# Two latent feed-forward norms rooted from sums that are gathered during the output projection, with the residual addition on GpSimd

## The reference, cut to what matters

```python
x = x + g1 * rmsnorm_2(y_lat, norm_g[l, 1])
x = x + g2 * rmsnorm_2(swiglu(modulate(x, norm_g[l, 2], sh2, sc2), ffn_w_in[l], ffn_w_out[l]),
                       norm_g[l, 3])
```

## Time and profile before

| | |
|---|---|
| median of 3 runs | 3146.11 us (3144.01 to 3150.38) |
| profiled execution, its own time | 3146.42 us |
| its span | 3144.5 us |
| busy PE; DVE; ACT; POOL | 3064.0 us (97%); 1814.2 (58%); 1188.8 (38%); 1241.6 (39%) |
| chain that ended last | PE 87%, DVE 8%, ACT 3%, issue 1%, POOL 1% |
| TensorE clock, mean | 0.99 of 2.4 GHz |

### The profile page before, as it was taken

The page is one execution under the profiler, slowest core; times in us unless marked ns, Lnnn a source line. Parts: engine busy times, 40 slices in busy tenths (PEclk is TensorE's granted clock), DMA queues, the critical chain, the costliest instruction groups (busy, mean ns, idle before and its releaser), DMA issues.

```text
span 3144.5 us, 41638 instructions
## 1 busy us (share of the span) xinstructions
PE 3064.0 (97%) x16512; PEld 2544.4 (81%) x16512; DVE 1814.2 (58%) x2858; ACT 1188.8 (38%) x1836; POOL 1241.6 (39%) x568
## 2 busy tenths in 40 slices
PE   8999999999999999999999999999999999999998
PEld 7658888886589888778888998878888788878887
DVE  3556777845553664666337877567786458352224
ACT  4544212235544432324336555542223435332222
POOL 4304444533157343334344454434444320134442
PEclk9999999999999999999999999999999999999999
DMA  7204554623135222223333333435653210123331
GB/s 130 77 14 118 169 164 129 196 67 82 36 111 167 87 75 88 80 67 108 108 101 101 111 113 106 134 111 171 191 160 117 82 61 14 41 71 100 98 95 67
DMA packets 480432, 323.87 MB, mean 103 GB/s; under 512 B 102520, under 2 KB 447744, under 8 KB 479728
## 3 DMA queue, kind: packets, MB, share of 16 engines
q1 hardware_dynamic: 475472, 309.60, 33.7%
q10 hardware_dynamic: 2656, 6.30, 0.5%
q0 software_dynamic: 2112, 5.32, 0.5%
HBM read 315.90 MB, written 5.24 MB: 102 GB/s over the span
## 4 chain that ended last, share of the span: by engine, by line
PE 87%; DVE 8%; ACT 3%; issue 1%; POOL 1%; DMA 0%; DVEq 0%; ACTq 0%; POOLq 0%
PE G L2854 13%; PE G L2863 12%; PE G L2864 12%; PE G L2868 12%; PE G L3082 6%; PE G L3083 5%; PE G L3087 5%; PE G L2880 3%; PE G L3944 1%; PE G L3299 1%; POOL WL L749 1%; PE SS L3210 1%; PE G L3236 1%; ACT WH L808 1%; PE G L3289 1%
## 5 line engine op out<-in xcount | busy, mean ns | idle before, releaser
L749 POOL TENSOR_TENSOR WL<-raw,WH 128x1024 fp32r<-128x1024 f32 (+1 forms) x520 | 1218.9, 2365 | 1796.8 <-ACT WH L808 1796.8
L808 ACT ACTIVATE WH<-raw 128x1024 fp32r<-128x1024 f32 (+1 forms) x520 | 492.1, 994 | 580.7 <-PE G L3087 397.1
L2863 PE MATMUL G<-hH,WH 128*128 128x512 f32 x1520 | 595.9, 392 | 0.0
L2864 PE MATMUL G<-hL,WH 128*128 128x512 f32 x1520 | 592.8, 390 | 0.0
L2868 PE MATMUL G<-hH,WL 128*128 128x512 f32 x1520 | 359.9, 389 | 0.0
L2863 PEld LDWEIGHTS G<-hH,WH 128*128 128x128 f32 x1520 | 285.9, 188 | 60.7 <-ACT t_s L1289 0.8
L2864 PEld LDWEIGHTS G<-hL,WH 128*128 128x128 f32 x1520 | 286.0, 188 | 58.8
L2868 PEld LDWEIGHTS G<-hH,WL 128*128 128x128 f32 x1520 | 285.3, 188 | 59.2
L1723 DVE SCALAR_TENSOR_TENSOR acc<-adaw,cvec,acc 128x512 f32<-128x512 f32 x280 | 250.8, 949 | 4.2
L2854 PE MATMUL G<-hH,WH 128*128 128x512 f32 (+1 forms) x432 | 166.9, 386 | 0.0
L2854 PE MATMUL G<-hL,WH 128*128 128x512 f32 (+1 forms) x432 | 164.3, 380 | 0.0
(11 more groups left out here) (777 smaller groups left out, 6197.2 us busy)
## 6 DMA issues: line engine op xcount, KB each, us to landing
raw<-ffn_w_in_in SPq DMA_DIRECT2D x264, 256.0 KB, 3.4
adaw<-ada_w_in SPq DMA_DIRECT2D x48, 1024.0 KB, 5.3
raw<-ab_w_in_in SPq DMA_DIRECT2D x128, 256.0 KB, 3.0
raw<-ffn_w_out_in SPq DMA_DIRECT2D x96, 256.0 KB, 2.9
raw<-w_gate_in SPq DMA_DIRECT2D x88, 256.0 KB, 3.3
raw<-w_up_in SPq DMA_DIRECT2D x88, 256.0 KB, 3.4
raw<-w_down_in SPq DMA_DIRECT2D x64, 256.0 KB, 2.8
raw<-w_in_in SPq DMA_DIRECT2D x40, 256.0 KB, 3.3
```

Of the source, the lines that this page charges most:

```text
L749: nc.gpsimd.tensor_tensor(WL[c % 2][:, cut], raw[c % 2][:, cut], WH[c % 2][:, cut].bitcast(F32), ALU.subtract)\
L808: nc.scalar.activation(WH[c % 2][:, cut], raw[c % 2][:, cut], ACT.Copy).then_inc(weights_hi, 1)
L2863: mm(dst, view(WH[c % 2], k), high, start=(k == 0 and not (joint and i)), stop=False)
L2864: mm(dst, view(WH[c % 2], k), low, start=False, stop=False)
```

## The change

It rewrites what stands between o7 and gu1 at both places:

- The three sums of the formula above are gathered while o0 to o7 are made. ACT squares y as before and also squares G y (`y1.c`, with the gain as scale); DVE multiplies x, gain and bank (`y1.b`) and adds the three running totals in PSUM banks (M[1], M[0], S[0]), for k = 1 to 6. `last_out` puts the column products of the totals (12 of the program's) into o7, ahead of its last three matmuls.
- `fresh_columns` adds the last tile's three column products behind o7, spreads the first root, does 8 keep-awake matmuls and spreads the second root. ACT takes the second root (`root_of_fresh`) from sums that DVE puts together in five 128 x 4 operations. sum x^2 (`squared_x`) is kept from the norm that each layer began with, by a copy.
- The new x is no longer needed for the sums. DVE makes the update tiles (`d1`), POOL adds them to xT (`fresh_rows`, between the low parts of gu0 and of gu1 in its order), DVE makes h and hL. The three are interleaved, two updates ahead.
- `opening` has no keep-awake matmuls of its own at the two places. At m the 32 transposes and 8 copies to xtok move into the opening, in two banks instead of four, and gu1 waits for the last copy. `late` (WH of gu1) moves ahead of the seventh tile.
- `rows_back` is issued ahead of the last head tiles. SP waits for POOL's eighth addition instead of `t.x1.7`.

```diff
@@ GpSimd
+            def fresh_rows(n):
+                for k in range(KD):
+                    pool.wait_ge(dve_done, at("dve", f"{n}.d1.{k}"))
+                    nc.gpsimd.tensor_tensor(xT[:, k, :], xT[:, k, :], ht[:, k % 2, :], ALU.add).then_inc(x_added, 1)
+            seam = first["t.o"] + 5
+            low_parts(cut2, seam)
+            fresh_rows("t")
+            low_parts(seam, cut3)
@@ SP
-                    sp.wait_ge(dve_done, at("dve", "t.x1.7"))
+                    sp.wait_ge(x_added, FRESH_ROWS["t"] + KD)
@@ ScalarE
+            def root_of_fresh(n):
+                act.wait_ge(dve_done, at("dve", f"{n}.n2.var"))
+                nc.scalar.activation(ncol[:, 12:16], squared_x[:, int(n == "m"), :], ACT.Sqrt, bias=eps[:, 0:1], scale=1.0 / D)\
+                    .then_inc(act_done, did("act", f"{n}.n2.root"))
@@ ScalarE, projected, behind the square of y
+                        if k >= 3:
+                            act.wait_ge(dve_done, at("dve", f"{n}.y1.cad{k - 2}"))
+                        nc.scalar.activation(five_rows[n][:, k % 2, :] if k else S[0][:, :], y[:, k, :], ACT.Square, scale=mcols[:, passes[n][0], 1, k:k + 1])\
+                            .then_inc(act_done, did("act", f"{n}.y1.c{k}"))
@@ ScalarE
+            rows_back()
             latent_heads()
-            projected("t", PT_.y, T, KD, ((1, rows_back),))
+            projected("t", PT_.y, T, KD)
@@ VectorE, fresh_sums
+                    V.scalar_tensor_tensor(product if k else M[0][:, :], x[:, k, :], gain(n, 1)(k), out_bank(n, k)[:, :], ALU.mult, ALU.mult)\
+                        .then_inc(dve_done, did("dve", f"{n}.y1.b{k}"))
+                    if inner:
+                        V.tensor_tensor(M[1][:, :] if k < KD - 2 else rstd[:, :], M[1][:, :], sq[:, k % 2, :], ALU.add)
+                        V.tensor_tensor(M[0][:, :] if k < KD - 2 else five_rows[n][:, 3, :], M[0][:, :], product, ALU.add)
+                        V.tensor_tensor(S[0][:, :] if k < KD - 2 else five_rows[n][:, 2, :], S[0][:, :], five_rows[n][:, k % 2, :], ALU.add)
@@ VectorE, fresh_normed
+                dve.wait_ge(pe_done, at("pe", f"{n}.y1.bc"))
+                update(0)
+                dve.wait_ge(act_done, at("act", f"{n}.n2.root"))
+                V.reciprocal(ncol[:, 8:12], ncol[:, 12:16]).then_inc(dve_done, did("dve", f"{n}.n2.rec"))
+                update(1)
+                dve.wait_ge(pe_done, at("pe", f"{n}.n2.bc"))
+                for k in range(KD):
+                    dve.wait_ge(x_added, FRESH_ROWS[n] + k + 1)
+                    if k >= 2:
+                        dve.wait_ge(dve_done, at("dve", f"{n}.n2.L{k - 2}"))
+                    V.scalar_tensor_tensor(scaled_rows(f"{n}.n2", ht, k, T), x[:, k, :], gx(k), S[0][:, :], ALU.mult, ALU.mult).then_inc(dve_done, did("dve", f"{n}.n2.h{k}"))
+                    if k + 2 < KD:
+                        update(k + 2)
+                    if k >= 1:
+                        rest(k - 1)
+                rest(KD - 1)
@@ TensorE, opening
-                keep_busy(n, 8)
+                if n not in ("t.n2", "m.n2"):
+                    keep_busy(n, 8)
...
+                    if n == "m.n2":
+                        turned_residual(k)
@@ TensorE
+            def fresh_columns(n):
+                keep_busy(f"{n}.y1", 4)
+                pe.wait_ge(act_done, at("act", f"{n}.y1.sq{KD - 1}"))
+                column_of(M[0], 0, sq[:, (KD - 1) % 2, :], False, True).then_inc(pe_done, did("pe", f"{n}.y1.sum"))
+                pe.wait_ge(dve_done, at("dve", f"{n}.y1.b{KD - 1}"))
+                column_of(S[1], 0, five_rows[n][:, 4, :], False, False)
+                pe.wait_ge(act_done, at("act", f"{n}.y1.c{KD - 1}"))
+                column_of(S[1], 4, five_rows[n][:, (KD - 1) % 2, :], False, True).then_inc(pe_done, did("pe", f"{n}.y1.sums"))
+                pe.wait_ge(dve_done, at("dve", f"{n}.y1.rec"))
+                to_all(M[1][:, :], 0).then_inc(pe_done, did("pe", f"{n}.y1.bc"))
+                keep_busy(f"{n}.n2", 8)
+                pe.wait_ge(dve_done, at("dve", f"{n}.n2.rec"))
+                to_all(S[0][:, :], 8).then_inc(pe_done, did("pe", f"{n}.n2.bc"))
```

More of the change, by code:

```diff
@@ L300, in __init__ @@
                 self.last, self.part = last, part
+                self.five_at = last - size([P, 5, N])
                 row = size([P, N])
@@ L852, in stats, with rounded @@
                 root(n, cols // P, K * P)
-            def rounded(n, K, H, free, cols=T, shift=None, k0=0, temp=ht, late=None):
+            def rounded(n, K, H, free, cols=T, shift=None, k0=0, temp=ht, late=None, late_at=None, then=None):
                 for k in range(k0, K):
-                    if k == (0 if n in IN_BANKS and n != "b0.n1" else 2) and late is not None:
+                    if k == (late_at or (0 if n in IN_BANKS and n != "b0.n1" else 2)) and late is not None:
                         hi(late)
@@ L865, in rounded @@
                         nc.scalar.activation(H[:, k, 0:cols], scaled_rows(n, temp, k, cols), ACT.Copy).then_inc(act_done, did("act", f"{n}.H{k}"))
+                    if then and k >= 2:
+                        then(k - 2)
+                if then:
+                    then(K - 2)
+                    then(K - 1)
             def feed_forward(n, silu=silu, N=T, between=iter(()), last=None):
@@ L1523, in second_half @@
                 n, N = ps.n, ps.N
[L1524 to L1536, removed]
+                root_of_fresh(n)
+                rounded(f"{n}.n2", KD, hH, f"{n}.o{KD - 1}", N, shift(n, 3), late=first[f"{n}.o"] + 5, late_at=6, then=kept_tokens if n == "m" else None)
                 feed_forward(n, ps.silu, N, between, (f"{n}.y2", lambda n, k: (ps.y2[:, k, :], lambda k: act.wait_ge(dve_done, at("dve", f"{n}.down3.{k}")))))
@@ L2353, in second_half @@
+            def second_half(ps, x, p, y1, between=iter(())):
                 n, N = ps.n, ps.N
-                mean(f"{n}.n2", N)
-                normed(f"{n}.n2", KD, lambda k: x[:, k, :], gain(p, 2), hH, hL, N, shift(p, 3))
+                fresh_sums(n, x)
+                fresh_normed(n, y1, x)
                 feed_forward(n, ps.y2, N, ps.FH, ps.FL, ps.silu, fresh=True, between=between, last=f"{n}.y2")
@@ L3043, in feed_forward @@
                         else:
+                            if n == "m" and t == 1:
+                                pe.wait_ge(act_done, at("act", f"m.xt{KD - 1}"))
                             streamed(c, groups)
```

120 lines of the change are left out of this document (93 added, 27 removed).

## The result

| | before | after |
|---|---|---|
| median | 3146.33 us (20 runs, 3142.49 to 3151.84) | 3151.91 us (20 runs, 3146.69 to 3155.76) |
| profiled execution; its span | 3146.42; 3144.5 | 3154.8; 3153.0 |
| ratio, 95% interval | | 1.0018 (1.0012 to 1.0024) |
| busy PE; DVE; ACT; POOL | 3064.0; 1814.2; 1188.8; 1241.6 | 3066.7; 1831.4; 1187.8; 1262.3 |
| chain that ended last | PE 87%, DVE 8%, ACT 3% | PE 88%, DVE 8%, ACT 2% |

What follows compares the result with a forecast made beforehand. PE, busy 97% of the span, was taken to bound the kernel. 8.6 - 0.2 + 6.5 - 1.3 - 0.3 = 13.3 us less than 3146.4 gave 3133, range 3129.5 to 3138.5.

Steps and rivals of the forecast that it cites:

- Equal times elsewhere: Outside the two places and the longer o7, the new profile would show the same times as before.
- 0.2 us at t, 1.3 at m: Loss from the lower clock in the openings after PE's wait: 0.2 us (at most 1) and 1.3 (0 to 3).
- 8.6 were forecast: Place t, o7's added products included: 28.0 us against 36.6, 8.6 us less, before the clock's loss.
- 6.5 ahead of the clock's 1.3: Place m, with transposes and copies in the opening: 30.8 us against 37.3, 6.5 less, before the clock's loss.
- The first h can start at 8.0: Behind o7 at each place: column products, two spreads and keep-awake products let DVE start the first h at 8.0 us.
- Inside o7, 2.5 us: Three groups of column products ahead of o7's last three matmuls cost 2.5 us on the path at each place.
- The cycle, 2.10: On DVE in the openings, one cycle of h, update, hL takes 2.10 us, bounds 1.98 and 2.34; before, 1.44.
- The mechanism at m: ACT's tile copies and WH make hH6 and hH7 late; gu1 waits for the last copy, at 28.3 us.
- POOL's additions at 1.27 us, not waited for, and DVE not slowed beside them: Eight additions of 1.27 us fit DVE's 2.1 us cycle; the rival of mutual blocking would give 3153.
- The old rows, 0.3 us: Rows fetched earlier shift ACT's queue and DVE's hL row ahead of t: 0.3 us lost, between 2 gained and 0.8 lost.
- SP's later release delays nothing: Released at about 22.8 us behind z instead of 17.5, gu2's weights still come in time, with 5 us cover.
- the clock stays at 1.2 GHz: Rival: low clock through the whole opening at both places, 8.3 us slower, 3154; most of slower's 0.04.

Runs made afterwards that it cites:

- e4: The changed kernel with its new 32-byte tile at the end of memory, every tile of before where it lay: 3138.73 us, ratio 0.9973.
- e1: The kernel before with one unused 32-byte tile ahead of the large tiles, no instruction differing: 3157.74 us, ratio 1.0034.
- e6: As e4, with 14 keep-awake products ahead of the opening at both places: 3136.23 us, ratio 0.9971.
- e7: As e4, with o7's 12 column products put one behind each of its last 12 matmuls: 3136.46 us, ratio 0.9975.
- e8: e6 and e7 together, with 4 keep-awake products instead of 8 between the two spreads: 3131.65 us, ratio 0.9956.
- e9: As e8, with the third update ahead of the first h: 3134.12 us, ratio 0.9959.
- e12: The kernel of e9 run once more, unchanged: 3135.65 us, ratio 0.9965.
- e10: As e4, with the residual additions on VectorE (DVE) instead of GpSimd, one ahead of each h: 3148.46 us, ratio 1.0013.
- e3: The changed kernel with 96 unused bytes behind its new tile, large tiles on multiples of 128 again: 3152.31 us, ratio 1.0016.

## Why the prediction was wrong, point by point

- **"Equal times elsewhere": wrong, and this turned the sign.** The new 32-byte tile was not priced at all. It cost 11 to 14 us (14 by the changed kernel's ratio 1.0018 against e4's 0.9973; 13.2 in the rows of the three untouched stretches; 10.7 when done alone, e1). With it taken out the kernel ran in 3138.7, just above the range's end.
- **The clock, "0.2 us at t, 1.3 at m": right for the openings, and the larger loss was missed.** It was put into the opening alone, behind PE's wait of 3.6 us. The wait came as predicted (3.57); at m the clock fell there and cost 1.7 us (e4 against e6), and at t, where it fell there in e7, it cost nothing. But the clock also fell ahead of the wait, under column products and spreads, where each microsecond of PE delays h0, and this stood in the sum at nothing. At t that made 12.55 of 8.0 in the changed kernel and in e4, and 9.7 in e6, with the clock low for a third of the time; at m it made 9.74, and 0.9 more in o7.
- **What the places missed, added up.** At t, 8.6 were forecast ahead of the clock's 0.2 and 2.8 came: 4.6 went to the late h0, 1.0 between h0 and gu1, 0.2 in o7. At m, 6.5 ahead of the clock's 1.3, and 1.8: 1.7 to the late h0, 1.9 between h0 and gu1, 1.1 in o7.
- **"The first h can start at 8.0": about right at the upper level of the clock, by an estimate.** No trace had eight keep-awake products and the clock up. In e8 the second spread starts 6.14 behind z at m; four keep-awake products more (half of the 1.95 of the earlier trace rows) make 7.1, and 1.1 from there to h0 (2062.58 to 2063.67 in e6) 8.2. By the prediction's own numbers PE asked for the second root 0.6 us after it was ready, behind eight keep-awake products; at the lower clock that became 1.9 (2060.64 to 2062.58 in e6).
- **Inside o7, 2.5 us: right at the upper level** (2.59 to the next matmul, 2.7 for o7 as a whole; 3.6 at m, where the clock fell), and putting the products between matmuls does not make it less (2.8 in e7).
- **The cycle, 2.10: 2.17** (2078.01 to 2080.18 on DVE), inside its bounds. Another 0.4 came in the middle, where 2.55 us lie between two hL (2083.67 to 2086.22) and DVE idles 0.48 ahead of the sixth h. WH of gu1 is not the cause, as ACT makes it only from 2086.28 on; what is, stays open. From h0 to gu1 the prediction had 17.5 us at t, and it took 18.5. At m it had 20.3; 22.2 in the changed kernel, 20.7 in e6 with the clock up.
- **The mechanism at m: right.** ACT's copies and WH delay the last tiles, and the last copy delays gu1:

```profile
2774.48 2.00 ACT L827 ACTIVATE WH<-raw 128x1024 fp32r<-128x1024 f32 x2
2776.38 0.68 ACT L890 ACTIVATE hH<-SS,mod 128x512 fp32r<-128x512 f32 x1
```

- **POOL's additions at 1.27 us, not waited for, and DVE not slowed beside them: right** (in the kernels with four keep-awake products between the spreads DVE does wait for the first addition: 0.73 us at m in e8, 0.66 at each place in e9 and e12). e10 shows what they are worth, 12.6 us. The Trainium skill (GPSIMD Engine Reference, section 4.1, Engine selection) would put them on VectorE, as GpSimd is about half as fast; here the slower engine had the time and the faster one did not (1.27 us on POOL against 0.69 on DVE).
- **The old rows, 0.3 us: nothing seen.** The critical hL pair ahead of place t still takes 5.05 us.
- **SP's later release delays nothing: right.** From gu1 of t to the start of o7 of m it took 645.7 us in e4 and 646.0 before.
- **The rival "the clock stays at 1.2 GHz"** named the right cause and the wrong stretch. No rival had the memory layout.

**The best version** is e8 or e9, which their intervals don't tell apart: 0.9956 to 0.9965 of before, 11 to 14 us faster, for the change with its new tile out of the way, keep-awake products where PE waits and fewer of them where PE is waited for. The intervals of e6 and e7 overlap with these. Open is what makes the clock stay up behind o7 in one execution and fall in the next, and with it 2 to 3 us at each place.

## What to carry to other kernels

A new buffer is an edit to every kernel line that reads a tile laid out behind it: put it at the end, or look at the mean ns of the untouched matmul groups before blaming the new code. When a stretch on PE is made shorter, ask of each instruction left in it whether it stands on the path; keep-awake products belong where PE waits, and not where an engine waits for PE. If the total says no and the rows say yes, do not drop the cause yet: make the experiment that parts them.

## What the runs showed of the hardware

- In the rows shown, a 128x512 down-projection matmul took 0.2267 us with its moving tile at a distance of 0 or 256 bytes (beyond a multiple of 256) from the weight tiles, 0.2289 at 64, 0.2322 at 128 and 0.2333 at 32. Moving all tiles together changed nothing.
- Twelve column products (128 x 128 rows against one column) cost 0.20 to 0.23 us each at the upper level, in one piece or between matmuls, and PE's busy share is full under them; yet under or right behind them the clock fell at place t in the changed kernel and in each of e3, e4, e6 to e10 and e12, for 3.4 to 10.2 us. In the five traces of the instructions of before it never fell there.
- A wait of 3.57 us without work left the clock at the upper level at place t of the changed kernel, of e3 and of e4 and at m of e7; it fell at m of the changed kernel, of e3 and of e4, and at t of e7 at 2069.0, just behind the wait (2064.3 to 2067.85). With keep-awake products in the wait it fell in none of eight.
